# Moving the SBUF addresses of a matmul kernel's operands: the weights' ring to a multiple of 512 bytes, each streamed buffer to an offset of its own

## The chip, the cores and the metric

The kernel is one program on one NeuronCore of a Trainium2 chip. The metric is the device time of one execution in microseconds (us). TensorE (PE) multiplies, ScalarE (ACT), VectorE (DVE) and GpSimd (POOL) do the elementwise work, SyncE (SP) issues most of the transfers.

## What is computed

The reference is two blocks of a small transformer, batch 1, 512 tokens, width 1024, everything in float32. Each of the first two layers does this:

```python
xn = rmsnorm(h, norm_g[i]);  proj = xn @ w_in[i]          # a recurrent mixer and a sparse attention read proj
h = h + concatenate([y_hg, y_nsa]) @ w_out[i]
gate = sigmoid(rmsnorm(h, ple_norm_g[i]) @ w_pg[i])
h = h + gate * (p[i] @ w_pp[i])
```

Then come two layers of the second block, each a feed-forward part, a mixer (differential attention in the first, pooling in the second), a cross attention to a memory of 256 tokens, and a second feed-forward part, with a layer norm after each:

```python
def swiglu_ffn(x, w_in, w_out):                           # D_FF = 2816
    h = x @ w_in
    g, u = jnp.split(h, 2, axis=-1)
    return (jax.nn.silu(g) * u) @ w_out
```

What matters for this change is that nearly all the work is a product of an activation of 512 tokens with a weight matrix, 464 slabs of weights of 128 x 1024 numbers in all.

## The kernel before

Activations lie transposed in SBUF (channel on the partition, token along it). `h` is the running activation, [128, 8, 512]. A float32 product is made as three products of the type float32r: every operand is split into a rounded high part and the low part that is left. The weights go through three rings of RING = 4 slots, 4096 bytes per partition each: SP loads a slab into `raw` (a transfer of 512 KB), ACT rounds it into `wh` (line 883), POOL writes the low part `wl` = raw - wh (line 319), and PE reads `wh` and `wl`. The activations are split into pairs: `xh`, `xl` ([128, 8, 512], the input of most products), `hh`, `hl` ([128, 22, 512], the hidden layer of the feed-forward part), `mh`, `ml` ([128, 8, 256], the memory).

All products go through `passes`, which the profile shows as three lines, L405, L407 and L409. Each issues two matmuls, of the left and the right half of a bank of 512 columns, so the order on PE is six matmuls with 256 moving columns, then the next six:

```python
for n, c in enumerate(parts):      # L405: weights wh, moving xh (or hh, mh)
    nc.tensor.matmul(dst[:, c], high_l, high_r[:, c], start=first and n == 0, stop=False)
for c in parts:                    # L407: weights wh, moving xl (or hl, ml)
    nc.tensor.matmul(dst[:, c], high_l, low_r[:, c], start=False, stop=False)
for n, c in enumerate(parts):      # L409: weights wl, moving xh (or hh, mh)
    out = nc.tensor.matmul(dst[:, c], low_l, high_r[:, c], start=False, ...)
```

Every matmul is led by its own load of 128 columns of weights (LDWEIGHTS, the rows of the engine PEld), which runs beside the matmul ahead of it. Six of these per 128 x 128 tile of weights make 48 per slab. In the stages that produce values with the token on the partition (`token_major`), the roles are swapped: `xh`, `xl`, `mh` or `ml` is the loaded operand, and the ring (`wh`, `wl`) is the streamed one, 256 columns wide or, in one stage of each of the first layers, 280.

The stages are in a fixed order that is written out by hand (`plan`), and engines wait for each other by semaphores. PE, ACT and POOL go two to four slabs ahead of each other within the ring. Between the products lie the stages of the mixers (plain float32 matmuls, other lines) and the norms, in which DVE, ACT and POOL work on `h`, `tb`, `sg`, `sq`, `s1`, `s2` and write `xh` and `xl` again (POOL line 333).

A tensor's place in SBUF isn't given in the code. It follows from the order of the `keep` calls: each tensor starts where the one before it ends, rounded up to 32 bytes, and the first one behind a scratch area of 16384 bytes and 128 bytes of constants. Tensors made by `views` are released again and are laid over by what follows, so `hh`/`hl`, `proj` and what follows it, `dq` and the others, `xq` to `xpt`, and `pooled` all begin at one address. Of each matmul operand the table gives the start (bytes from the partition's start) and what is left of it after division by 512; each slot, each tile of weights (512 bytes) and each half of a bank (1024 bytes) has the same remainder as its buffer.

| buffer | start before | rest of 512 before | start after | rest of 512 after |
|---|---|---|---|---|
| h | 16512 | 128 | 4096 | 0 |
| raw | 32896 | 128 | 20480 | 0 |
| wh | 49280 | 128 | 36864 | 0 |
| wl | 65664 | 128 | 53248 | 0 |
| sg, tb, sq, s1, s2 | 86368 and on | 352 | 73952 and on | 224 |
| xh | 104512 | 64 | 92192 | 32 |
| xl | 120896 | 64 | 108640 | 96 |
| hh | 137280 | 64 | 125568 | 128 |
| hl | 182336 | 64 | 170752 | 256 |
| mh | 178240 | 64 | 166720 | 320 |
| ml | 186432 | 64 | 174976 | 384 |

Of the kernel before, what the change touches and what calls it, by code (L numbers as in the profile page):

```python
# [25 lines left out]
P = 128  # L26
T = 512
TT = T // P
D = 1024
KC = D // P  # L30
DEPTH = 2
NF = 22
MEM = 256
# [131 lines left out]
def program(nc, x_t, slabs, prm1, prm2, consts, rot2, rope, masks, cmp_tab, spread, causal, w1, pp_w, p_t,  # L165
            pool_w, mem_t, positions, out):
    f32, f32r, bf16, i32 = mybir.dt.float32, mybir.dt.float32r, mybir.dt.bfloat16, mybir.dt.int32
# [6 lines left out]
    with ctx:  # L174
        def keep(name, shape, dt=f32):
            return ctx.enter_context(nc.sbuf_tensor(name, shape, dt))
# [2 lines left out]
            return ctx.enter_context(nc.semaphore(name))  # L179


        h = keep("h", [P, KC, T])
        raw = keep("raw", [P, RING, D])
        wh = keep("wh", [P, RING, D], f32r)
# [15 lines left out]
        ksm = keep("ksm", [P, 3, 64])  # L200
        lbt = keep("lbt", [P, 4, 4])
        lam = keep("lam", [P, 4])


        def views(specs):
            made = []
            with ExitStack() as scope:
                for name, shape, dt in specs:
                    made.append(scope.enter_context(nc.sbuf_tensor(name, shape, dt)))
            return made  # L210


        with nc.sbuf_tensor("x_room", [P, 2 * KC * T], f32):
# [9 lines left out]
                                    ("pct", [P, 2, T], f32)])  # L223

        (dpa, dpt) = views([("dpa", [P, 3, 1280], f32), ("dpt", [P, 2, TT, T], f32)])
        xh, xl = keep("xh", [P, KC, T], f32r), keep("xl", [P, KC, T], f32r)

        (proj, vt, vgt, rop, msk, cmt, side, spr) = views([
            ("proj", [P, NPROJ, T], f32), ("vt", [P, TT, T], f32), ("vgt", [P, TT, VG], f32),
# [3 lines left out]
            ("dq", [P, KC, T], f32), ("dk", [P, KC, T], f32), ("dkz", [P, 2, KC, T], f32), ("dv", [P, TT, D], f32),  # L233
            ("drop", [P, 2, T], f32), ("dspr", [16, 8 * P], f32)])
        (dpos,) = views([("dpos", [P, T], i32)])
        (xq, xk, xv, xm, mh, ml, xpa, xpt) = views([
            ("xq", [P, KC, T], f32), ("xk", [P, KC, MEM], f32), ("xv", [P, MT, D], f32),
            ("xm", [P, KC, MEM], f32), ("mh", [P, KC, MEM], f32r), ("ml", [P, KC, MEM], f32r),
            ("xpa", [P, 2, TT, MEM], f32), ("xpt", [P, 2, MT, T], f32)])

        (pooled, _, pside) = views([("pooled", [P, KC, T], f32), ("memory_room", [P, 5 * KC * MEM], f32),
                                    ("pside", [P, 16, P], f32)])
        hh, hl = keep("hh", [P, NF, T], f32r), keep("hl", [P, NF, T], f32r)
        pin = vt
        tot_a = proj[:, KCM:KCM + 2, :].rearrange("p a t -> p (a t)").rearrange("p (h t) -> p h t", h=4)
        tot_b = sq[:, 0, :].rearrange("p (h t) -> p h t", h=4)
# [1725 lines left out]
```

## Time and profile before

| | |
|---|---|
| time, median of 3 runs | 3622.61 us |
| the 3 runs | 3620.0, 3622.61, 3631.73 us |
| the profiled execution's own time | 3616.13 us |
| its span, first to last instruction | 3614.3 us |
| PE busy | 3243.3 us, 90% |
| PEld busy | 2907.5 us, 80% |
| POOL, DVE, ACT busy | 1369.7, 1251.1, 1105.5 us |
| mean granted clock of TensorE | 0.946 of 2.4 GHz |
| moved by DMA | 261.86 MB, 72 GB/s over the span |

The busy time of an engine counts the time in which at least one of its instructions runs. Matmuls overlap in the records, so a matmul's duration (276 ns, say) is longer than the time from its start to the start of the next, and it's this second time that adds up to the span. In a stretch where PE never stops, it's the stretch divided by the number of matmuls.

### The profile page before, as it was taken

The numbers are of one execution on the slowest core, as the hardware profiler recorded it, in microseconds if no ns is written. First come the engines' busy times: TensorE is split into PE (matmuls) and PEld (weight loads), VectorE is DVE, ScalarE is ACT, GpSimd is POOL, SyncE is SP. The second block draws the span as 40 slices with busy tenths as digits, with TensorE's granted clock in tenths as the row PEclk, the third lists the DMA queues.
The fourth block names the chain that finished last, engine by engine and source line by source line (L and its number), as shares of the span: only waits on it lengthen the run. The fifth ranks groups of instructions, "written<-read, shape, count | busy, mean of one in ns | idle before, by whom it ended". The sixth has DMA issues, their size and how long they took to land.

```text
span 3614.3 us, 59291 instructions
## 1 busy us (share of the span) xinstructions
PE 3243.3 (90%) x24262; PEld 2907.5 (80%) x24262; DVE 1251.1 (35%) x2127; ACT 1105.5 (31%) x1835; POOL 1369.7 (38%) x651
## 2 busy tenths in 40 slices
PE   5988898997799899989788898999899987889997
PEld 5985476997358899979447878999799975789997
DVE  2026654106564311050576053110411058251103
ACT  2232433222253322132253333221322233332222
POOL 4433014443103344444403624444444444244442
PEclk9988899998799999999898999999999998999999
DMA  4320012331001232313101412222232331213231
GB/s 160 93 70 18 1 30 76 96 102 36 6 1 59 77 99 93 99 57 105 35 1 58 134 46 74 92 93 96 64 99 93 100 101 57 70 60 101 95 99 53
DMA packets 72068, 261.86 MB, mean 72 GB/s; under 512 B 7920, under 2 KB 8560, under 8 KB 70800
## 3 DMA queue, kind: packets, MB, share of 16 engines
q1 hardware_dynamic: 70048, 250.32, 21.8%
q10 hardware_dynamic: 1904, 9.94, 0.8%
q8 instruction: 79, 1.29, 0.1%
q14 instruction: 37, 0.30, 0.0%
HBM read 258.13 MB, written 2.10 MB: 72 GB/s over the span
## 4 chain that ended last, share of the span: by engine, by line
PE 77%; DVE 15%; ACT 3%; issue 3%; POOL 1%; DMA 0%; SPq 0%; DVEq 0%; ACTq 0%; POOLq 0%
PE bank L405 22%; PE bank L409 21%; PE bank L407 21%; PE bank L644 2%; PE bank L670 2%; DVE tb L1352 1%; PE bank L635 1%; DVE sg L1341 1%; PE bank L582 1%; PE bank L818 1%; DVE s L1302 1%; ACT wh L883 1%; PE bank L576 1%; PE bank L508 1%; DVE proj L1464 1%
## 5 line engine op out<-in xcount | busy, mean ns | idle before, releaser
L319 POOL TENSOR_TENSOR wl<-raw,wh 128x1024 fp32r<-128x1024 f32 x464 | 1153.9, 2503 | 1876.3 <-ACT wh L883 1876.2
L405 PE MATMUL bank<-xh,wh 128*128 128x256 f32 x5120 | 1017.4, 280 | 106.8 <-POOL xl L333 77.6
L407 PE MATMUL bank<-xl,wh 128*128 128x256 f32 x5120 | 1010.5, 279 | 0.0
L409 PE MATMUL bank<-xh,wl 128*128 128x256 f32 x5120 | 1009.7, 279 | 0.0
L405 PEld LDWEIGHTS bank<-xh,wh 128*128 128x128 f32 x5120 | 783.5, 190 | 124.1 <-issue 94.3
L883 ACT CAST wh<-raw 128x1024 fp32r<-128x1024 f32 x464 | 468.3, 1047 | 1043.4 <-PE bank L409 1010.6
L407 PEld LDWEIGHTS bank<-xl,wh 128*128 128x128 f32 x5120 | 783.7, 190 | 0.0
L409 PEld LDWEIGHTS bank<-xh,wl 128*128 128x128 f32 x5120 | 781.9, 190 | 0.0
L405 PE MATMUL bank<-hh,wh 128*128 (+1 forms) x1408 | 279.3, 280 | 5.8 <-ACT sg L1132 5.8
L409 PE MATMUL bank<-hh,wl 128*128 (+1 forms) x1408 | 279.3, 280 | 0.0
L407 PE MATMUL bank<-hl,wh 128*128 (+1 forms) x1408 | 279.0, 280 | 0.0
L1630 DVE TENSOR_TENSOR tb<-sg,bank 128x512 f32<-128x512 f32 x88 | 60.5, 687 | 616.7 <-ACT sg L1132 616.7
L1132 ACT ACTIVATE sg<-bank 128x512 f32<-128x512 f32 x88 | 52.7, 598 | 685.6 <-PE bank L409 685.6
L1584 DVE SCALAR_TENSOR_TENSOR h<-h,bank 128x512 f32<-128x512 f32 x72 | 49.5, 687 | 512.7 <-PE bank L409 511.0
L405 PEld LDWEIGHTS bank<-hh,wh 128*128 128x128 f32 x1408 | 215.3, 189 | 6.5 <-ACT sg L1132 6.5
L409 PEld LDWEIGHTS bank<-hh,wl 128*128 128x128 f32 x1408 | 215.4, 189 | 0.0
L407 PEld LDWEIGHTS bank<-hl,wh 128*128 128x128 f32 x1408 | 214.4, 188 | 0.0
L1632 DVE TENSOR_TENSOR hl<-tb,hh 128x512 f32 x88 | 123.7, 1405 | 161.9 <-ACT hh L1136 161.9
L1546 DVE TENSOR_REDUCE small<-bank 128x1 f32<-128x128 f32 (+1 forms) x224 | 106.7, 476 | 81.3 <-PE bank L645 73.8
L1370 DVE COPY proj<-bank 128x512 f32 x28 | 19.4, 692 | 293.2 <-PE bank L409 293.2
L644 PE MATMUL bank<-proj 128*128 128x128 f32 (+3 forms) x256 | 89.1, 471 | 11.7 <-DVE proj L1513 11.4
L333 POOL TENSOR_TENSOR xl<-h,xh 128x512 fp32r<-128x512 f32 x48 | 73.3, 1538 | 62.2 <-ACT xh L937 61.6
(301 smaller groups left out, 3613.3 us busy)
## 6 DMA issues: line engine op xcount, KB each, us to landing
raw<-in_slabs SPq DMA_DIRECT2D x464, 512.0 KB, 3.5
h<-in_x_t SPq DMA_DIRECT2D x1, 2048.0 KB, 8.4
w1v<-in_w ACTq DMA_DIRECT2D x2, 1024.0 KB, 4.8
side<-in_pp_w ACTq DMA_DIRECT2D x2, 1024.0 KB, 4.8
xm<-in_mem_t ACTq DMA_DIRECT2D x2, 1024.0 KB, 4.8
out<-h SPq DMA_DIRECT2D x8, 256.0 KB, 2.0
side<-in_w SPq DMA_DIRECT2D x1, 1024.0 KB, 14.2
vt<-in_p_t ACTq DMA_DIRECT2D x2, 512.0 KB, 3.6
```

The costliest lines, as they stand in the source:

```text
L319: nc.gpsimd.tensor_tensor(wl[:, n % RING, :], raw[:, n % RING, :], wh[:, n % RING, :], A.subtract).then_inc(w_low, 1)
L333: nc.gpsimd.tensor_tensor(xl[:, c, :], h[:, c, :] if st["kind"] == "ln" else tb[:, c % 2, :], xh[:, c, :], A.subtract).then_inc(S["xl"], 1)
L405: nc.tensor.matmul(dst[:, c], high_l, high_r[:, c], start=first and n == 0, stop=False)
L407: nc.tensor.matmul(dst[:, c], high_l, low_r[:, c], start=False, stop=False)
L409: out = nc.tensor.matmul(dst[:, c], low_l, high_r[:, c], start=False, stop=last and n == len(parts) - 1)
L644: nc.tensor.matmul(bank[t][:, 0:w], q[:, t * P:w], k[:, 0:w], start=True, stop=False)
L670: last = nc.tensor.matmul(o[:, k * P:T], vgt[:, k, col:col + 64], ptt[:, u % 2, k, k * P:T], start=False, stop=(br == 1 and k == TT - 1))
L883: nc.scalar.copy(wh[:, slot, :], raw[:, slot, :]).then_inc(w_high, 1)
L1132: nc.scalar.activation(sg[:, j, :], bank[2 * j][:], F.Silu).then_inc(took_a, 1)
L1546: step(V.tensor_reduce(small[:, 0, u % 2, t:t + 1], bank[t][:, 0:w(t)], AX, A.max))
L1630: V.tensor_tensor(tb[:, j, :], sg[:, j, :], bank[2 * j + 1][:], A.mult).then_inc(took_v, 1)
L1632: V.tensor_tensor(flat(hl[:, bass.ds(i * 2 + j, 1), :]), tb[:, j, :], flat(hh[:, bass.ds(i * 2 + j, 1), :]), A.subtract).then_inc(S["hl"], 1)
```

## The change

No instruction is added, removed or moved on any engine, and no operand changes its shape or type. Only addresses change. The scratch area shrinks from 16384 to 2048 bytes; pads are put ahead of `h` (1920 bytes), behind `lam` (64), ahead of `xh` (32), `xl` (64), `hh` (128), `hl` (128), `mh` (320) and `ml` (64), and behind `xl` (416). The ring and `h` come to multiples of 512, and the six streamed buffers to the six offsets of the table above. The buffers of the mixers (`proj`, `hk`, `dq` and so on) go from 64 to 0 bytes above a multiple of 512.

```diff
+        keep("fore_room", [P, 2048 - 128], mybir.dt.uint8)
         h = keep("h", [P, KC, T])
         raw = keep("raw", [P, RING, D])
         wh = keep("wh", [P, RING, D], f32r)
...
         lam = keep("lam", [P, 4])
+        keep("mid_room", [P, 64], mybir.dt.uint8)
...
-        xh, xl = keep("xh", [P, KC, T], f32r), keep("xl", [P, KC, T], f32r)
+        u8 = mybir.dt.uint8
+        keep("xh_room", [P, 32], u8)
+        xh = keep("xh", [P, KC, T], f32r)
+        keep("xl_room", [P, 64], u8)
+        xl = keep("xl", [P, KC, T], f32r)
+        keep("x_end", [P, 512 - 96], u8)
...
-        (xq, xk, xv, xm, mh, ml, xpa, xpt) = views([
+        (xq, xk, xv, xm, _, mh, _, ml, xpa, xpt) = views([
             ("xq", [P, KC, T], f32), ("xk", [P, KC, MEM], f32), ("xv", [P, MT, D], f32),
-            ("xm", [P, KC, MEM], f32), ("mh", [P, KC, MEM], f32r), ("ml", [P, KC, MEM], f32r),
+            ("xm", [P, KC, MEM], f32), ("mh_room", [P, 320], u8), ("mh", [P, KC, MEM], f32r),
+            ("ml_room", [P, 64], u8), ("ml", [P, KC, MEM], f32r),
...
-        (pooled, _, pside) = views([("pooled", [P, KC, T], f32), ("memory_room", [P, 5 * KC * MEM], f32),
+        (pooled, _, pside) = views([("pooled", [P, KC, T], f32), ("memory_room", [P, 5 * KC * MEM + 96], f32),
...
-        hh, hl = keep("hh", [P, NF, T], f32r), keep("hl", [P, NF, T], f32r)
+        keep("hh_room", [P, 128], u8)
+        hh = keep("hh", [P, NF, T], f32r)
+        keep("hl_room", [P, 128], u8)
+        hl = keep("hl", [P, NF, T], f32r)
...
-    nc = bacc.Bacc("TRN2", target_bir_lowering=False, num_devices=1)
+    nc = bacc.Bacc("TRN2", target_bir_lowering=False, num_devices=1, dynamic_dma_scratch_size=2048)
```

## Rows read from the trace of the kernel before

**Rows 1.** The profile's page: busy times, and the chain that ended last
```profile
PE 3243.3 (90%) x24262; PEld 2907.5 (80%) x24262; DVE 1251.1 (35%) x2127; ACT 1105.5 (31%) x1835; POOL 1369.7 (38%) x651
...
PE 77%; DVE 15%; ACT 3%; issue 3%; POOL 1%; DMA 0%; SPq 0%; DVEq 0%; ACTq 0%; POOLq 0%
PE bank L405 22%; PE bank L409 21%; PE bank L407 21%; PE bank L644 2%; PE bank L670 2%; DVE tb L1352 1%; PE bank L635 1%; DVE sg L1341 1%; PE bank L582 1%; PE bank L818 1%; DVE s L1302 1%; ACT wh L883 1%; PE bank L576 1%; PE bank L508 1%; DVE proj L1464 1%
```

**Rows 2.** Groups on PE: xcount, busy us, mean ns of one, idle before
```profile
L405 PE MATMUL bank<-xh,wh 128*128 128x256 f32 x5120 | 1017.4, 280 | 106.8 <-POOL xl L333 77.6 <-DVE xl L1312 21.4 <-ACT vgt L973 4.5
...
L405 PE MATMUL bank<-hh,wh 128*128 (+1 forms) x1408 | 279.3, 280 | 5.8 <-ACT sg L1132 5.8
...
L405 PE MATMUL bank<-wh,xh 128*128 128x256 f32 (+1 forms) x320 | 72.0, 291 | 22.7 <-POOL xl L333 13.3 <-ACT vt L973 4.5 <-ACT dk L962 2.6
...
L405 PE MATMUL bank<-mh,wh 128*128 128x256 f32 x128 | 38.3, 299 | 20.2 <-POOL ml L393 10.7 <-POOL wl L319 5.7 <-ACT xq L962 3.1
...
L405 PE MATMUL bank<-wh,mh 128*128 128x256 f32 x128 | 27.3, 296 | 6.7 <-ACT xq L962 2.6 <-ACT xk L962 2.4 <-ACT xv L973 1.6
```

**Rows 3.** Windows inside feed-forward stages: length, busy us (xcount), granted clock
```profile
1460.00:1570.00 110.00, 110.00 (x937) 110.00 (x935) 3.00 (x5) 21.24 (x21) 45.77 (x20) 1.00 0.32 98
2200.00:2430.00 230.00, 230.00 (x1955) 230.00 (x1954) 41.79 (x40) 59.97 (x80) 104.08 (x40) 1.00 0.30 93
...
2600.00:2810.00 210.00, 210.00 (x1855) 210.00 (x1855) 40.32 (x39) 58.21 (x78) 98.95 (x38) 1.00 0.30 97
2825.00:2935.00 110.00, 110.00 (x973) 110.00 (x972) 6.25 (x10) 22.24 (x23) 47.08 (x20) 1.00 0.31 100
```

**Rows 4.** Timeline of PE in two stages with the same buffers: start, length
```profile
1499.92 0.40 PE L409 MATMUL bank<-hh,wl 128*128 x2
1500.16 0.40 PE L405 MATMUL bank<-hh,wh 128*128 x2
1500.39 0.40 PE L407 MATMUL bank<-hl,wh 128*128 x2
...
2900.06 0.39 PE L405 MATMUL bank<-hh,wh 128*128 x2
2900.29 0.39 PE L407 MATMUL bank<-hl,wh 128*128 x2
2900.51 0.39 PE L409 MATMUL bank<-hh,wl 128*128 x2
```

**Rows 5.** Windows over the stretches at the longer spacing, PE's count first
```profile
38.70:81.00 42.30, 37.96 (x288) 37.56 (x288) 9.44 (x10) 13.87 (x18) 26.37 (x15) 0.93 0.33 102
500.00:608.00 108.00, 104.02 (x798) 95.80 (x798) 50.12 (x52) 35.54 (x50) 44.65 (x22) 1.00 0.22 69
629.00:672.00 43.00, 38.32 (x291) 37.95 (x292) 9.53 (x10) 13.86 (x18) 27.06 (x16) 0.93 0.35 104
1455.00:1582.00 127.00, 126.54 (x1061) 125.32 (x1062) 16.17 (x23) 26.49 (x30) 50.73 (x21) 1.00 0.28 87
1722.00:1747.00 25.00, 22.88 (x192) 22.68 (x192) 1.38 (x2) 5.21 (x6) 16.49 (x7) 1.00 0.27 85
2047.00:2077.00 30.00, 26.30 (x200) 25.71 (x201) 1.83 (x4) 11.07 (x13) 22.88 (x10) 0.94 0.52 166
2190.00:2432.00 242.00, 240.54 (x2042) 240.37 (x2042) 44.58 (x43) 65.68 (x88) 110.47 (x44) 1.00 0.29 91
2432.00:2560.00 128.00, 127.55 (x1064) 125.68 (x1064) 16.15 (x23) 27.46 (x31) 50.71 (x22) 1.00 0.27 87
3466.00:3594.00 128.00, 127.53 (x1063) 125.83 (x1064) 16.16 (x23) 26.32 (x30) 48.33 (x20) 1.00 0.21 66
```

**Rows 6.** Other matmuls: min/median/max ns; first one with 64 moving columns
```profile
L523 PE MATMUL bank<-prm,hidv x8: 275/275/323, 278.4 to 871.7; 128*128 128x64 f32 x8
...
L635 PE MATMUL bank<-cst,pa x320: 272/273/329, 393.2 to 1087.5; 128*128 128x128 f32 x160
```

**Rows 7.** Two stretches of one token-major stage, where the roles are swapped
```profile
L409 PE MATMUL bank<-wh,xl 128*128 128x256 f32 x59 | 11.6, 276 | 0.0
...
L405 PE MATMUL bank<-wh,xh 128*128 128x256 f32 x62 | 12.4, 281 | 2.2 <-ACT dv L973 2.2
```

**Rows 8.** The ring's work, its waits and its transfers
```profile
L319 POOL TENSOR_TENSOR wl<-raw,wh 128x1024 fp32r<-128x1024 f32 x464 | 1153.9, 2503 | 1876.3 <-ACT wh L883 1876.2
...
L883 ACT CAST wh<-raw 128x1024 fp32r<-128x1024 f32 x464 | 468.3, 1047 | 1043.4 <-PE bank L409 1010.6
...
L333 POOL TENSOR_TENSOR xl<-h,xh 128x512 fp32r<-128x512 f32 x48 | 73.3, 1538 | 62.2 <-ACT xh L937 61.6
...
raw<-in_slabs SPq DMA_DIRECT2D x464, 512.0 KB, 3.5
```

## The prediction

> **What bounds the kernel now.** I read the page first. The chain that ended last is PE for 77%, and three lines, L405, L407 and L409, hold 64% of it [rows 1]. The groups of PE say what these are: 5120 + 1408 + 320 + 128 + 128 = 7104 matmuls on each of the three lines, 21,312 in all, nearly all with 256 moving columns, a mean duration of 280 ns, and little idle time ahead of them [rows 2]. So next I asked how far apart they start. In a window in which PE is busy throughout, that's length over count. The first and the last window of [rows 3] both lie inside a stage that makes the output of a feed-forward part: the same code, the same buffers `hh`, `hl`, `wh`, `wl`, the same granted clock of 1.00. Yet one has 937 matmuls in 110 us (117.4 ns each), the other 973 (113.1 ns). The timeline shows the same thing as a steady pace: two matmuls in 0.235 us in the first, in 0.225 us in the second [rows 4]. The two windows between them give 230 / 1955 = 117.6 and 210 / 1855 = 113.2 ns for the stages that read `xh` and `xl` [rows 3]. There are two levels, 4.4 ns apart, and a stage stays on one for hundreds of matmuls, up to two thousand.
>
> Most of the longer level lies in the nine stretches of [rows 5]. Their counts add up to 288 + 798 + 291 + 1061 + 192 + 200 + 2042 + 1064 + 1063 = 6999, about one third of the 21,312. They hold a few others, and a few short stretches are not in them, which I leave out. So the longer level costs 7000 x 4.4 = **31 us** now, and the other 14,300 would cost **63 us** more if they were on it too.
>
> Everything else about the ring is covered. POOL waits 1876 us for ACT, ACT 1011 us for PE, and a slab's load lands in 3.5 us, where PE takes 48 x 113 ns = 5.4 us for a slab, with four slots between them [rows 8].
>
> **The change, part by part.** No instruction comes or goes, so no term comes from a count. There are four terms, each a changed duration.
>
> *The products with the ring as weights* (5120 + 1408 + 128 on each line, 94% of the 21,312). Before, the two operands that PE reads at a time lie at 128 and 64 bytes above a multiple of 512. They are the same in every stage, and both levels occur with them. So the addresses alone don't select the level; what PE did before must. What the trace can't show is what happens at other distances, as it has only one here. It bears on it in one place: in the token-major stages the roles are swapped, and with them the sign of the distance (the loaded operand at 64, the streamed one at 128). There the durations are 276 and 281 ns, again within one stage [rows 7], and 276 and 281 are what the two levels give in the products. A distance of +64 behaves as one of -64. The change makes the distance (streamed minus ring) 32, 96, 128, 256, 320 and 384. The bounds for this term:
> - Below: the matmul with 64 moving columns still takes 275 ns [rows 6], when its streaming is a quarter as long. Something other than the streaming sets that, and the load of 128 columns of weights is what it shares with the 256-column ones. 275 against 276 leaves 1 ns, with rounding up to 1.7 ns per matmul. The 128-column transposes at 272 ns [rows 6] are a different kind of load, and I don't count on them. So the most that a change of address could give is all on the lower level, 31 us, and 21,312 x 1.6 = 34 us below it, 65 us in all.
> - Above: all on the longer level, +63 us. A third level further up is possible, but none of the 256-column rows shows one.
>
> My value lies between. At present all operands of a stage have equal remainders, so the six matmuls of `passes` repeat with nothing that differs, and a stage that starts at the longer level has nothing that could bring it out (1061, 1064 and 1063 matmuls in a row, [rows 5]). With `xh` and `xl` 64 bytes apart, and `hh` and `hl` 128, the sequence has two changes in six. That can end a bad pace, or a good one. As two thirds are on the lower level now, it seems the more easily reached of the two. And the loaded and the streamed operand come further apart for all but `xh` (32). I take it that a bit more than half of what is lost on the longer level comes back: the share falls from 33% to 15%, or 3800 matmuls x 4.4 ns = **-17 us**.
>
> *The token-major products* (6%, 1344 matmuls): the streamed ring is at 0, the weights at 32, 96, 320, 384. The same bounds, -1 to +6 us; 0 taken.
>
> *The work on DVE, ACT and POOL*: their operands go from 128, 64 and 352 to 0 and the like, 224, 32 and 96. Nothing in the trace ties a duration to an address. POOL's `xl` takes 1538 ns [rows 8], and PE waits 77.6 us in all for it [rows 2]. A change of 10% either way in all of them is 7 us; 0 taken. If `wl` (2503 ns) took 10% more, it would still be hidden: two slabs take 5.5 us of POOL and 10.9 of PE.
>
> *Transfers*: `raw` goes to a multiple of 512. The ring's loads are hidden by the two loads that are ahead. 0. The shorter scratch area takes nothing away, as no queue of POOL's moves data.
>
> The sum is -17 us. Against the profiled execution it's 3616 - 17 = 3599; that one is 6.5 us below the median of the three runs, so against the median it's 3622.6 - 17 = **3606 us**.
>
> **What the skill says to this.** [...] The Trainium skill, "SBUF — State Buffer", section "Who interferes with whom", has PE with two independent read ports, and says "PE and ACT never wait on anyone"; its section on operand start alignment asks only for a multiple of the element's size, and adds that this is about legality and that nothing was timed. By this rule both layouts are alike and the time is 3622.6: it's the first rival below. [...]
>
> **The rivals.**
> - *Addresses don't matter* (0.30). For it: both levels at equal addresses, and no change with the sign of the distance. Then each stage draws its level anew from how it starts. A stage like the feed-forward output is 1063 x 4.4 = 4.7 us either way, so a few of them give +-10 us, about the spread of the three runs (11.7 us). Time 3622, between 3612 and 3633.
> - *The unequal offsets keep knocking PE off the lower level* (0.28). This is the case on the slower side. The lower level needs equal conditions from one matmul to the next, it's now held for 1855 matmuls in a row [rows 3], and a change of remainder twice in six ends it. All at the longer level gives 3622.6 + 63 = 3685; half of the lower ones gives 3654. It decides as soon as the share at the longer level is over 45%, where it's 33% now: each tenth of the 21,312 is 9.4 us, and 0.3% of the time (about what a measurement of this kernel can tell from no change) is 11 us.
> - *Below the lower level* (0.10): the new distances remove what's left above the weights' load. 3622.6 - 65 = 3558, if everywhere.
> - The forecast itself (0.32): 3591 with all on the lower level to 3611.
>
> **How the numbers follow.** The chance of faster by over 0.3% is 0.32 + 0.10 = 0.42, of slower 0.28, of no change 0.30. The likeliest case is 3606, its own range 3591 to 3611. As cases of both signs hold much, the range goes from 3560, where the lower rival is nearly whole, to 3676, close to the end of the upper one, and leaves some 0.07 below and 0.09 above it.
>
> **What the profile of the changed kernel would show.** Right: the mean duration of the L405, L407 and L409 groups falls from 280 towards 277 ns, and the windows of feed-forward stages hold 970 matmuls in 110 us, not 937, in at least three of the four. The groups with `xh`, `hh` and `mh` may then differ from each other, as they have different offsets; were they alike, the offset would not be the cause. If addresses don't matter, windows of both counts are seen again, at other places, and the means stay near 280. If unequal offsets hurt, windows of 937 are all over, or there is a pace between the two. A mean below 276 would be the third case. What would make me wrong in another way: a duration on DVE or POOL that moves by over 5%, a ring that no longer keeps up (PE waiting for `wl` L319, which it does for next to nothing now), or a changed granted clock.

## The result, and the profile after

The changed kernel takes **3676.6 us** (median of 4 runs, 3674.98 to 3680.52), against 3627.17 for the kernel before in the same rounds (3620.0 to 3647.14). The ratio is 1.0129, interval 1.0086 to 1.0172 (it compares all the runs, so it isn't the quotient of the two medians): slower by 1.3%. The forecast of 3606 has the wrong sign, and the time lies 0.6 us above the end of the range. The profiled execution is 3674.98 us with a span of 3673.2, 58.9 us more than before.

The page of the changed kernel: busy times, the chain by engine, and the groups that answer to [rows 2] and [rows 8] (xcount, busy us, mean ns | idle before). The edits move the three lines of the products from L405, L407, L409 to L416, L418, L420.

```profile
PE 3305.6 (90%) x24262; PEld 2969.6 (81%) x24262; DVE 1248.7 (34%) x2127; ACT 1105.0 (30%) x1835; POOL 1369.0 (37%) x651
...
PE 76%; DVE 15%; issue 4%; ACT 3%; POOL 1%; DMA 0%; SPq 0%; DVEq 0%; ACTq 0%; POOLq 0%
...
L330 POOL TENSOR_TENSOR wl<-raw,wh 128x1024 fp32r<-128x1024 f32 x464 | 1152.9, 2501 | 1935.1 <-ACT wh L894 1935.1
L416 PE MATMUL bank<-xh,wh 128*128 128x256 f32 x5120 | 1030.3, 283 | 104.6 <-POOL xl L344 76.1
...
L416 PE MATMUL bank<-hh,wh 128*128 (+1 forms) x1408 | 281.5, 281 | 5.8 <-ACT sg L1143 5.8
```

Only PE has changed: 3243.3 before [rows 1], 3305.6 now, which is 62.3 us more of a span that grew by 58.9. DVE, ACT and POOL have moved by 2.4 us at most; `wl` takes 2501 ns where it took 2503 [rows 8]; PE's wait for `xl` is 76.1 us where it was 77.6 [rows 2]. The 59 us that POOL waits longer for ACT are PE's, handed on through the ring.

The windows inside three stages (length, PE busy with its count) answer to [rows 3]: the first is a feed-forward output, the second reads `xh` and `xl`, the third is the output that was at the lower level before.

```profile
1490.00:1600.00 110.00, 110.00 (x934) 110.00 (x933) 7.54 (x11) 21.42 (x22) 43.02 (x18) 1.00 0.28 91
2620.00:2830.00 210.00, 208.42 (x1770) 208.21 (x1769) 39.20 (x39) 58.41 (x78) 96.38 (x38) 1.00 0.29 90
2870.00:2980.00 110.00, 110.00 (x933) 110.00 (x933) 2.64 (x4) 21.20 (x21) 45.70 (x20) 1.00 0.32 98
```

No feed-forward stage holds 973 any more: 110 / 933 is 117.9 ns and 208.42 / 1770 is 117.8. (A window also counts the two or three matmuls that run across its edges, so the quotient comes out some 0.2 ns below the distance of the starts: 110 / 973 is 113.1 where the starts are 113.3 apart.) The clock is 1.00 as before, so this is no throttle. The timeline shows what a pace of this kind looks like inside (start, length of a pair):

```profile
1300.06 0.40 PE L416 MATMUL bank<-xh,wh 128*128 128x256 f32 x2
1300.29 0.40 PE L418 MATMUL bank<-xl,wh 128*128 128x256 f32 x2
1300.53 0.41 PE L420 MATMUL bank<-xh,wl 128*128 128x256 f32 x2
```

Taken one matmul at a time it isn't the old longer level. These are the distances from one start to the next, in ns, in a stage with `xh` and `xl`, in the kernel before and in the changed one (differences of start times, 18 of each):

```
before  118 117 118 118 117 119 117 118 118 118 117 118 118 117 119 117 118 118
after   116 117 117 128 120 115 120 115 116 118 118 116 117 118 117 116 119 117
```

Before, the steps are even. After, they are uneven (115 to 128), the 18 repeat as a group, and they sum to 2120 ns, a mean of 117.78. The old longer level sums to 2120 too, so the mean alone doesn't tell the two apart.

### The profile page after: what moved, and what is told of

Same layout as the page of the kernel before. It is cut to its first block, busy times and chain, and to the rows that moved or that the text cites. A ratio compares the mean times of both kernels' runs of the same rounds, so it can differ in the third digit from the quotient of the medians.

```text
span 3673.2 us, 59291 instructions
## 1 busy us (share of the span) xinstructions
PE 3305.6 (90%) x24262; PEld 2969.6 (81%) x24262; DVE 1248.7 (34%) x2127; ACT 1105.0 (30%) x1835; POOL 1369.0 (37%) x651
## 4 chain that ended last, share of the span: by engine, by line
PE 76%; DVE 15%; issue 4%; ACT 3%; POOL 1%; DMA 0%; SPq 0%; DVEq 0%; ACTq 0%; POOLq 0%
PE bank L420 21%; PE bank L416 21%; PE bank L418 21%; PE bank L655 2%; PE bank L681 2%; DVE tb L1363 1%; PE bank L646 1%; DVE sg L1352 1%; PE bank L593 1%; ACT wh L894 1%; PE bank L829 1%; PE bank L587 1%; DVE s L1313 1%; PE bank L519 1%; DVE proj L1475 1%
## 5 line engine op out<-in xcount | busy, mean ns | idle before, releaser
L330 POOL TENSOR_TENSOR wl<-raw,wh 128x1024 fp32r<-128x1024 f32 x464 | 1152.9, 2501 | 1935.1 <-ACT wh L894 1935.1
L416 PE MATMUL bank<-xh,wh 128*128 128x256 f32 x5120 | 1030.3, 283 | 104.6 <-POOL xl L344 76.1
L420 PE MATMUL bank<-xh,wl 128*128 128x256 f32 x5120 | 1036.3, 284 | 0.0
L418 PE MATMUL bank<-xl,wh 128*128 128x256 f32 x5120 | 1020.9, 281 | 0.0
L416 PEld LDWEIGHTS bank<-xh,wh 128*128 128x128 f32 x5120 | 795.2, 190 | 122.6 <-issue 96.3
L420 PEld LDWEIGHTS bank<-xh,wl 128*128 128x128 f32 x5120 | 790.8, 190 | 0.0
L418 PEld LDWEIGHTS bank<-xl,wh 128*128 128x128 f32 x5120 | 789.2, 190 | 0.0
L416 PE MATMUL bank<-hh,wh 128*128 (+1 forms) x1408 | 281.5, 281 | 5.8 <-ACT sg L1143 5.8
L420 PE MATMUL bank<-hh,wl 128*128 (+1 forms) x1408 | 281.4, 282 | 0.0
L418 PE MATMUL bank<-hl,wh 128*128 (+1 forms) x1408 | 279.7, 280 | 0.0
L416 PEld LDWEIGHTS bank<-hh,wh 128*128 128x128 f32 x1408 | 216.1, 188 | 6.5 <-ACT sg L1143 6.5
L418 PEld LDWEIGHTS bank<-hl,wh 128*128 128x128 f32 x1408 | 216.2, 188 | 0.0
L420 PEld LDWEIGHTS bank<-hh,wl 128*128 128x128 f32 x1408 | 215.0, 189 | 0.0
```

The costliest lines, as they stand in the source:

```text
L330: nc.gpsimd.tensor_tensor(wl[:, n % RING, :], raw[:, n % RING, :], wh[:, n % RING, :], A.subtract).then_inc(w_low, 1)
```

## The experiments

All change addresses alone, by the size of pads. xl_alone and wl_alone have the remainders of the kernel before, but the changed kernel's short scratch area and its place for the mixers' buffers; wl128_only alone is built on the kernel before, all others on the changed one. "Distance" is the start of the streamed operand minus that of the loaded one. Remainders are those by 512. `passes` reads (`wh`, `xh`), (`wh`, `xl`) and (`wl`, `xh`), two matmuls of each in turn. The pace is window length over count, or the mean difference of start times inside a stage where no window is shown (differences of 150 ns and more, which are waits, left out). It's that of the profiled execution; where this one lies at an end of a kernel's runs, the text says so. The x, h and m stages are those that stream `xh`/`xl`, `hh`/`hl` and `mh`/`ml`. There are 18 x stages, four h stages (feed-forward outputs) and two m stages, and between them six token-major ones. The layouts, and what they took (the four scans and odd16 have two runs each):

| kernel | wh, wl | xh, xl | hh, hl | mh, ml | median us | ratio to before, interval |
|---|---|---|---|---|---|---|
| changed | 0, 0 | 32, 96 | 128, 256 | 320, 384 | 3676.6 | 1.0129 [1.0086, 1.0172] |
| equal_pairs | 0, 0 | 32, 32 | 128, 128 | 320, 320 | 3671.0 | 1.0106 [1.0051, 1.0160] |
| all_zero | 0, 0 | 0, 0 | 0, 0 | 0, 0 | 3714.0 | 1.0226 [1.0171, 1.0281] |
| xl_alone | 128, 128 | 64, 128 | 64, 64 | 64, 64 | 3661.5 | 1.0110 [1.0075, 1.0145] |
| wl_alone | 128, 192 | 64, 64 | 64, 64 | 64, 64 | 3656.6 | 1.0090 [1.0057, 1.0123] |
| scan_a | 0, 0 | 256, 256 | 192, 192 | 384, 384 | 3699.6 | 1.0200 [1.0101, 1.0300] |
| scan_b | 0, 0 | 160, 160 | 96, 96 | 480, 480 | 3697.4 | 1.0194 [1.0099, 1.0290] |
| scan_c | 0, 0 | 224, 224 | 384, 384 | 352, 352 | 3687.6 | 1.0167 [1.0071, 1.0263] |
| scan_d | 0, 0 | 64, 64 | 288, 288 | 416, 416 | 3666.2 | 1.0108 [1.0013, 1.0203] |
| odd16 | 0, 0 | 80, 80 | 48, 48 | 64, 64 | 3704.6 | 1.0215 [1.0153, 1.0277] |
| all_64 | 0, 0 | 64, 64 | 64, 64 | 64, 64 | 3664.0 | 1.0104 [1.0056, 1.0151] |
| all_192 | 0, 0 | 192, 192 | 192, 192 | 192, 192 | 3623.5 | 1.0001 [0.9972, 1.0029] |
| same_class | 0, 0 | 64, 192 | 64, 320 | 64, 448 | 3666.5 | 1.0110 [1.0065, 1.0155] |
| wl_class | 0, 128 | 64, 64 | 64, 192 | 192, 64 | 3600.7 | 0.9931 [0.9911, 0.9951] |
| wl128_64 | 0, 128 | 64, 64 | 64, 64 | 64, 64 | 3588.0 | 0.9883 [0.9846, 0.9920] |
| wl128_192 | 0, 128 | 192, 192 | 192, 192 | 192, 192 | 3588.3 | 0.9884 [0.9847, 0.9920] |
| wl128_only | 128, 256 | 64, 64 | 64, 64 | 64, 64 | 3586.9 | 0.9880 [0.9843, 0.9916] |

The first theory behind the result was that of the slower rival: inequality within a streamed pair does it. The first rival to it: the distance does it.

**equal_pairs**: the distances of `xh`, `hh` and `mh` stay, and each pair becomes equal.

```diff
         xh = keep("xh", [P, KC, T], f32r)
-        keep("xl_room", [P, 64], u8)
         xl = keep("xl", [P, KC, T], f32r)
...
         hh = keep("hh", [P, NF, T], f32r)
-        keep("hl_room", [P, 128], u8)
         hl = keep("hl", [P, NF, T], f32r)
```

> The new layout with the two buffers of each pair at one offset again: xh and xl at 32, hh and hl at 128, mh and ml at 320 bytes, the ring at 0. Theory (the unequal offsets inside a pair knock TensorE off its repeating pace): both levels of the kernel before return, stages at 113.3 or 117.8 ns from start to start, each constant over a stage, and the time is 3600 to 3640 us. Rival 1 (the distance from the ring sets the pace): the stages stay near 117.8 (xh) and 118.1 (hh) with matmuls of unequal spacing, time 3670 to 3680. Rival 2 (the move of the other buffers, the scratch area or h costs it): 3670 to 3680 too, but with the even spacing of the kernel before.

3671.0 us (3669.75 to 3672.8). The windows are of an x stage, an h stage and another x stage:

```profile
100.00:200.00 100.00, 100.00 (x859) 100.00 (x859) 6.22 (x9) 22.32 (x27) 42.14 (x19) 1.00 0.30 94
1500.00:1590.00 90.00, 90.00 (x761) 90.00 (x760) 2.27 (x4) 17.02 (x17) 37.17 (x16) 1.00 0.30 93
...
2250.00:2400.00 150.00, 150.00 (x1276) 150.00 (x1275) 28.50 (x27) 38.98 (x52) 70.87 (x28) 1.00 0.30 92
```

100 / 859 is 116.4 and 90 / 761 is 118.3; from the start times the first two stages have 116.7 and 118.67. The lower level doesn't return, and the theory that inequality alone does it falls. The h stages are slower than any h or x stage before. The third window, 150 / 1276, lies in an x stage at 117.8 by its start times: thirteen of the 18 x stages have 116.7 or 116.8, five 117.6 to 117.8. So a distance of 32 has two paces too, and a stage draws one of them.

**all_zero**: every remainder 0.

```diff
-        keep("xh_room", [P, 32], u8)
         xh = keep("xh", [P, KC, T], f32r)
-        keep("xl_room", [P, 64], u8)
         xl = keep("xl", [P, KC, T], f32r)
-        keep("x_end", [P, 512 - 96], u8)
```

> Everything at a multiple of 512 bytes: the ring and all six streamed buffers at 0, so that the distance is nothing and the offsets are equal. Theory (only unequal offsets cost): two even levels, 3600 to 3640 us, as with equal pairs. Rival (the distance from the ring matters by itself, and two operands at one offset collide most): a level above 118 ns in all products, 3690 us or more.

3714.0 us (3713.5 to 3715.07), the slowest of all. Window of an x stage, one of an h stage, and one of a later x stage:

```profile
100.00:200.00 100.00, 100.00 (x836) 100.00 (x835) 6.23 (x9) 21.55 (x26) 39.28 (x18) 1.00 0.31 94
...
1500.00:1600.00 100.00, 100.00 (x836) 100.00 (x835) 0.00 (x0) 18.85 (x18) 41.33 (x18) 1.00 0.31 96
2300.00:2400.00 100.00, 100.00 (x835) 100.00 (x835) 17.50 (x17) 25.90 (x35) 43.32 (x18) 1.00 0.31 94
```

They are 119.6 and 119.8 (100 / 836 and 100 / 835), and the starts are 120 ns apart, even to the nanosecond in most stages. With nothing unequal, distance 0 alone costs 6.7 ns a matmul over the lower level.

**xl_alone and wl_alone**: the ring at 128 and the streamed buffers at 64, as before, but `xl` or `wl` shifted by 64 bytes. The lines show that shift alone, for both kernels; the pads that keep the other buffers at their remainders are left out.

```diff
         xh = keep("xh", [P, KC, T], f32r)
+        keep("xl_room", [P, 64], mybir.dt.uint8)     # xl_alone
         xl = keep("xl", [P, KC, T], f32r)
...
         wh = keep("wh", [P, RING, D], f32r)
+        keep("wl_room", [P, 64], mybir.dt.uint8)     # wl_alone
         wl = keep("wl", [P, RING, D], f32r)
```

> The offsets of the kernel before (ring 128, all streamed buffers 64), and xl alone 64 bytes further, at 128, which is also the ring's own offset. Theory: the products on xh and xl go to a mean of 117.8 ns with uneven spacing at once, those on hh and hl stay on 113.3 or 117.8 with even spacing; time 3655 to 3675 us. Rival (distance): only the line that streams xl changes its pace, and the time moves by a third of that.

> The offsets of the kernel before, and wl alone 64 bytes further, at 192, so that the streamed buffers keep equal offsets and only the loaded ones differ, two of six in each repeat. If the load's address takes part in the pace, the products leave the two even levels, as with unequal streamed buffers: 3650 us or more. If only the streamed operand's address does, the products stay on 113.3 or 117.8 ns, only the token-major stages (6% of the matmuls), which stream wh and wl, change, and the time is 3600 to 3640 us.

3661.5 (10 runs, 3651.64 to 3668.29) and 3656.6 (10 runs, 3654.51 to 3658.42). With `xl` shifted, every x stage is at 117.24 and uneven, and the h stages, whose addresses relative to the ring are those of before, have 113.35 three times and 117.78 once. (The profile is that of the fastest of the ten runs, 10 us under their median; two h stages more on the longer level would be 9 us, so the other runs may have fewer on the lower one.) With `wl` shifted, x and h stages all have 116.7. Window of an h stage of each, xl_alone's first:

```profile
1480.00:1590.00 110.00, 110.00 (x973) 110.00 (x972) 6.07 (x10) 21.30 (x21) 48.16 (x20) 1.00 0.33 101
```

```profile
2460.00:2570.00 110.00, 110.00 (x946) 110.00 (x945) 4.87 (x8) 21.10 (x21) 45.31 (x19) 1.00 0.31 96
```

The loss follows the shifted buffer, and a shift of a loaded operand costs the lower level as one of a streamed operand does. So it's the relation of the two that counts, not where the streamed buffer lies by itself.

**The scan (scan_a to scan_d, odd16)**: pairs equal, ring at 0, so each stage measures one distance. The edit is the pad ahead of the pair; scan_a's is shown, the others differ in the numbers of the table (odd16 starts each tile 16 bytes in).

```diff
-        keep("xh_room", [P, 32], u8)
+        keep("xh_room", [P, 256], mybir.dt.uint8)
...
-        keep("hh_room", [P, 128], u8)
+        keep("hh_room", [P, 192], mybir.dt.uint8)
...
-            ("xm", [P, KC, MEM], f32), ("mh_room", [P, 320], u8), ("mh", [P, KC, MEM], f32r),
-            ("ml_room", [P, 64], u8), ("ml", [P, KC, MEM], f32r),
+            ("xm", [P, KC, MEM], f32), ("mh_room", [P, 384], u8), ("mh", [P, KC, MEM], f32r),
+            ("ml_room", [P, 512], u8), ("ml", [P, KC, MEM], f32r),
```

> The ring at 0 and equal offsets inside each pair: xh, xl at 256, hh, hl at 192, mh, ml at 384. Distance theory, as it stands after the first four runs (the pace is a function of streamed minus loaded offset modulo 512: 120.0 ns at 0, 116.7 at 32, 118.7 at 128, 113.3 or 117.8 at +64 and -64, 117.8 at 320, 113.3 at 192): each pair has one pace of its own in all its stages; the hh stages at 192 have 113.3, with some stages at 117.8; xh at 256, the furthest there is, at or below 113.3. Rival (colliding only near 0, the rest is how a stage starts): all three pairs at 113.3 or 117.8.

> As before with xh, xl at 160, hh, hl at 96, mh, ml at 480. Distance theory: 96 and 160 lie between neighbours at 113.3 to 118.7 and are odd multiples of 32, as 32 is, which had an uneven pace of 116.7 to 117.6: 116 to 118 ns for both, in every stage. Rival: 113.3 or 117.8 by stage.

> As before with xh, xl at 224, hh, hl at 384, mh, ml at 352. Distance theory: 384 is -128; if the sign doesn't matter, as it didn't for 64, 118.7 ns; 224 an odd multiple of 32, 116 to 118 ns. Rival: 113.3 or 117.8 by stage.

> As before with xh, xl at 64, hh, hl at 288, mh, ml at 416. Distance theory: xh at 64 has the two levels of the kernel before (there -64 in the products and +64 in the token-major stages), 113.3 and 117.8 by stage; 288 an odd multiple of 32, 116 to 118 ns. Rival (the ring's or h's own place, not the distance): xh at 64 is uneven too.

> Ring at 0, equal pairs at offsets that are odd multiples of 16 bytes, which the padding of the allocator never gives: xh, xl at 80 and hh, hl at 48, beside the cheap 64 (mh, ml at 64). If the pace depends on the distance in steps of 16 bytes with a minimum at 64, both lie between their neighbours (48 between 116.7 and 113.3, 80 between 113.3 and 120.0). If the steps are 32 or 64 bytes, 80 equals 64 and 48 equals 32. A pace below 113.3 is open: no run has looked there.

Several of these expectations missed: 256 has 120.0 and not 113.3 or less, 96 has 120.0 and 160 up to 118.7 where 116 to 118 was expected, and 48 lies above both its neighbours. Paces by distance, with the stage that gave each ("or" where the stages of one distance fall on two paces):

| distance | pace, ns | and 256 further | pace, ns |
|---|---|---|---|
| 0 | 120.0 (all_zero) | 256 | 120.0 (scan_a x) |
| 32 | 116.7 or 117.8 (equal_pairs x) | 288 | 116.7, once 117.8 (scan_d h) |
| 48 | 118.3 (odd16 h) | | |
| 64 | 113.3 or 117.8 (all_64) | 320 | 117.8 to 117.9 (equal_pairs m) |
| 80 | 118.3 or 120.0, some between (odd16 x) | | |
| 96 | 120.0 (scan_b h) | 352 | 120.0 to 120.1 (scan_c m) |
| 128 | 118.67 (equal_pairs h) | 384 | 118.67 (scan_c h) |
| 160 | 117.3 in three stages, 118.5 to 118.8 in the rest (scan_b x) | 416 | 118.1 to 118.8 (scan_d m) |
| 192 | 113.3 or 117.8 (all_192) | | |
| 224 | 118.3 (scan_c x) | 480 | 118.3 to 118.4 (scan_b m) |

To read two of them off the profile, a window in an x stage of scan_a (distance 256, 100 / 835 = 119.8) and of scan_b (distance 160, 100 / 855 = 117.0, one of the three stages at 117.3):

```profile
100.00:200.00 100.00, 100.00 (x835) 100.00 (x835) 5.67 (x9) 20.09 (x25) 40.14 (x17) 1.00 0.31 95
```

```profile
100.00:200.00 100.00, 100.00 (x855) 100.00 (x854) 6.23 (x9) 22.32 (x27) 41.48 (x19) 1.00 0.30 94
```

In every pair 256 apart the two agree within what a distance scatters by itself (320 was seen in two short stages alone). So what counts is the distance modulo **256**, not 512. The cheap ones are 64 and 192; the kernel before had 64 - 128, which is 192 by this measure, and the change left it for 32, 96, 128 and 256 in the x and h stages. No distance went below 113.3.

In all of these the ring is at 0, so the streamed buffer's own place would fit them as well. The token-major stages settle it, as there the ring is streamed and the buffer loaded, and the distance changes its sign. Windows of the token-major stage ahead of the differential attention: scan_a (distance 0 - 256), scan_c (0 - 224, which is 32) and scan_d (0 - 64, which is 192):

```profile
1740.00:1760.00 20.00, 20.00 (x169) 20.00 (x169) 0.00 (x0) 3.14 (x3) 7.72 (x4) 1.00 0.35 104
...
1729.00:1749.00 20.00, 20.00 (x174) 20.00 (x173) 0.00 (x0) 3.15 (x3) 8.84 (x4) 1.00 0.36 106
...
1750.00:1770.00 20.00, 20.00 (x179) 20.00 (x178) 0.00 (x0) 3.16 (x3) 14.24 (x6) 1.00 0.26 80
```

From the start times they have 119.9, 116.7 and 113.4, the paces of 0, 32 and 192 in the table. The others agree: 0 - 384 (128) has 118.7, 0 - 416 (96) 120.0, 0 - 32 (224) 118.3. So it's the streamed operand's start minus the loaded one's, whichever buffer plays which part.

**all_64 and all_192**: is 64 as good as 192?

```diff
-        keep("xh_room", [P, 32], u8)
+        keep("xh_room", [P, 64], mybir.dt.uint8)     # all_64; 192 in all_192
         xh = keep("xh", [P, KC, T], f32r)
-        keep("xl_room", [P, 64], u8)
         xl = keep("xl", [P, KC, T], f32r)
```

> The new layout in every way (ring and h at 0, short scratch area, all pads) but with all six streamed buffers at 64. Theory (what costs the time is the distance of the streamed from the loaded operand, modulo 256 bytes, and 64 and 192 are its cheapest values): each stage is back on 113.3 or 117.8 ns, evenly, and the time is that of the kernel before within its own scatter, 3594 to 3650 us. Rival (something else of the layout costs part of it): above 3655 us.

> The new layout with all six streamed buffers at 192, that is 64 bytes below the ring's offset modulo 256, as in the kernel before, where all at 64 was 64 above it. If the sign decides how often a stage lands on the upper level (products at -64: a third of the matmuls in the kernel before; at +64, in the run with all at 64: nearly all), the products on xh and xl are at 113.3 ns in most stages and the time is that of the kernel before, 3600 to 3645 us. If the sign doesn't matter and something else of the new layout does, the time is near 3664 us, as with all at 64.

3664.0 us (4 runs, 3659.38 to 3671.38) and 3623.5 (10 runs, 3613.97 to 3641.96): the ranges don't touch. Both levels occur in each, but all_64 draws the longer one in 16 of 18 x stages and three of four h stages, all_192 the lower one in half of its x stages and three of four h stages. The time of all_64 is the one that its rival named, that something else of the new layout costs; all_192 rules that out. Two h stages of all_192 and one of all_64 (110 / 973 = 113.1, 110 / 937 = 117.4):

```profile
1470.00:1580.00 110.00, 110.00 (x973) 110.00 (x972) 6.49 (x10) 22.58 (x23) 46.39 (x20) 1.00 0.32 100
...
2450.00:2560.00 110.00, 110.00 (x937) 110.00 (x936) 2.25 (x5) 21.18 (x21) 46.62 (x20) 1.00 0.32 100
```

```profile
1480.00:1590.00 110.00, 110.00 (x936) 110.00 (x935) 2.85 (x5) 21.17 (x21) 46.06 (x20) 1.00 0.31 98
```

all_192 has the changed kernel's smaller scratch area, its ring at 0 and its moved mixers' buffers, and its time is that of before (1.0001 [0.9972, 1.0029]). So the rest of the change costs nothing beyond some 0.3%.

**same_class and wl_class**: inequality with cheap distances alone. In same_class `xh` and `xl` are at 64 and 192, `hh` and `hl` differ by 256. In wl_class the loaded pair is at 0 and 128, with an equal x pair and an unequal h pair.

```diff
         xh = keep("xh", [P, KC, T], f32r)
-        keep("xl_room", [P, 64], u8)
+        keep("xl_room", [P, 128], mybir.dt.uint8)    # same_class; none in wl_class
         xl = keep("xl", [P, KC, T], f32r)
...
         wh = keep("wh", [P, RING, D], f32r)
+        keep("wl_room", [P, 128], mybir.dt.uint8)    # wl_class alone
         wl = keep("wl", [P, RING, D], f32r)
```

> Ring at 0, unequal pairs whose distances are all cheap ones: xh 64 and xl 192, hh 64 and hl 320, mh 64 and ml 448. Knocking theory (unequal offsets cost by themselves): xh/xl leave the two even levels, 116 to 118 ns in all stages; hh/hl differ by 256 bytes, the period of the distance, so they stay on 113.3 or 117.8. Time 3640 to 3670 us. Pure distance theory: both pairs stay on 113.3 or 117.8 by stage, time 3594 to 3650 us.

> wh at 0 and wl at 128, xh and xl at 64, hh 64 and hl 192, mh 192 and ml 64, so that every streamed operand is 64 bytes above or below every loaded one, modulo 256. Pure distance theory: 113.3 or 117.8 ns in every stage, 3594 to 3650 us. Knocking theory: uneven spacing everywhere, a mean near 116.7 as with wl alone, 3650 to 3670 us. An outcome below 113.3 or with no stage at 117.8 would be a way to gain.

3666.5 us (4 runs, 3661.57 to 3666.7) and 3600.7 (10 runs, 3598.77 to 3614.03). Both profiles are of a run at the end of its range: same_class's of the fastest, 5 us under the median, wl_class's of the slowest, 13 us above it. Two h stages of same_class, then an x stage and an h stage of wl_class:

```profile
1485.00:1595.00 110.00, 110.00 (x936) 110.00 (x935) 5.21 (x8) 20.48 (x21) 45.30 (x19) 1.00 0.30 95
...
2470.00:2580.00 110.00, 110.00 (x973) 110.00 (x972) 8.12 (x12) 22.06 (x23) 45.58 (x19) 1.00 0.32 96
```

```profile
2200.00:2400.00 200.00, 200.00 (x1767) 200.00 (x1766) 37.88 (x37) 54.03 (x72) 96.33 (x37) 1.00 0.31 97
...
1460.00:1570.00 110.00, 110.00 (x936) 110.00 (x936) 3.05 (x5) 21.18 (x21) 45.95 (x20) 1.00 0.31 98
```

In same_class every x stage has 117.8 in uneven steps (114 to 122), as in the changed kernel, although each distance by itself can have 113.3; its h stages, equal modulo 256, have 113.3 in three of four. So inequality does keep PE off the lower level: the slower rival was half right. And wl_class, meant as the mirror of it, showed something else: with `wl` 128 bytes off `wh` and an equal streamed pair, every x stage of the kernel has the lower level (200 / 1767 = 113.2; 113.3 to 114.1 by the starts), while its unequal h pair has 117.5 (110 / 936; 117.8 in uneven steps by the starts) in all four stages of the profiled run. As the median run is 13 us faster, that needn't be so in every run. Its m stages, whose streamed pair is unequal the other way round (192 and 64), have 120.9, more than distance 0 gives; why isn't known.

The token-major stages of same_class are the same case with the roles swapped, `xh` and `xl` loaded, 128 bytes apart, and an equal streamed ring. They are on the lower level throughout, 113.7 from the start times where all the matmuls are 256 columns wide; this is the one that has 119.4 in the changed kernel:

```profile
1750.00:1770.00 20.00, 20.00 (x179) 20.00 (x178) 0.00 (x0) 3.17 (x3) 14.26 (x6) 1.00 0.25 80
```

**wl128_64, wl128_192 and wl128_only**: the loaded pair 128 apart, every streamed pair equal. The first two are on the changed kernel; the third is the kernel before with two pads and nothing else.

```diff
         wh = keep("wh", [P, RING, D], f32r)
+        keep("wl_room", [P, 128], mybir.dt.uint8)
         wl = keep("wl", [P, RING, D], f32r)
...
         lam = keep("lam", [P, 4])
+        keep("lam_end", [P, 512 - 128], mybir.dt.uint8)
```

> wh at 0, wl at 128, all six streamed buffers at 64 (equal pairs). The run with hh at 64 and hl at 192 had every product on xh and xl at 113.4 ns and every product on hh and hl at 117.8. Theory (loaded operands 128 bytes apart and streamed ones equal leave the lower level as the only stable pace): the four feed-forward output stages also go to 113.4, 4224 matmuls by 4.4 ns or 19 us less than that run: 3575 to 3590 us. Rival (what helped was something of the xh buffers' own place): hh and hl stay at 117.8, 3600 us.

> The mirror image: wh at 0, wl at 128, all six streamed buffers at 192, so that wh is the one at a distance of -64 and wl at +64 (modulo 256). If only the loaded operands' being 128 apart counts: all products at 113.4 ns, 3575 to 3590 us. If the order of the signs over the six matmuls counts (four with wh, two with wl): another pace, or two levels again.

> The kernel before with one pad: wl 128 bytes further (256 above a multiple of 512, wh at 128, all streamed at 64), and 384 bytes behind lam to keep all that follows at its offsets. Distances -64 for wh, +64 for wl modulo 256, as in the mirror image. Theory: all products at 113.4 ns in every stage, 3575 to 3595 us, and less scatter between runs than the kernel before (3594 to 3651). Rival: the two levels stay, 3594 to 3650 us.

3588.0, 3588.3 and **3586.9 us** (3585.69 to 3587.54): 1.2% faster than the kernel before, and the changed kernel stands 3676.6 / 3586.9 = 2.5% above it. The groups of wl128_only, then its windows in three h stages and two x stages:

```profile
L407 PE MATMUL bank<-xh,wh 128*128 128x256 f32 x5120 | 1012.9, 279 | 105.5 <-POOL xl L335 76.4
L409 PE MATMUL bank<-xl,wh 128*128 128x256 f32 x5120 | 1007.3, 278 | 0.0
...
L407 PE MATMUL bank<-hh,wh 128*128 (+1 forms) x1408 | 274.3, 276 | 5.8 <-ACT sg L1134 5.8
```

```profile
2200.00:2430.00 230.00, 228.54 (x2016) 228.38 (x2016) 43.01 (x42) 63.04 (x83) 109.33 (x43) 1.00 0.31 99
2620.00:2830.00 210.00, 208.55 (x1841) 208.38 (x1840) 36.68 (x36) 56.26 (x73) 100.70 (x39) 1.00 0.31 97
...
1455.00:1565.00 110.00, 110.00 (x973) 110.00 (x973) 6.04 (x10) 21.82 (x22) 47.34 (x20) 1.00 0.32 101
2415.00:2525.00 110.00, 110.00 (x973) 110.00 (x972) 6.07 (x10) 21.27 (x21) 48.23 (x20) 1.00 0.33 101
2800.00:2910.00 110.00, 110.00 (x973) 110.00 (x972) 6.08 (x10) 21.29 (x21) 48.35 (x21) 1.00 0.32 101
```

All stages with the ring as weights have 113.3 to 114.0 from the start times (the window at 2415 us lies in the stage that [rows 5] has at 2432 us, on the longer level), and the hh group is at 276 ns where it was 280. PE's busy time is 3214.5 us, 28.8 under before. By the start times, 26 us of it come from the x and h stages, and the token-major ones give back 2, as the ring that they stream is now the unequal pair (117.7 to 118.0, and 121.8 where a third of the matmuls is 280 columns wide). The rest lies in the mixers' stages, whose PE time differs by some us from one profile to the next. The other two kernels have the same paces, but for the two short m stages of wl128_64, each of which holds the lower level in its first half and 118.9 in uneven steps in its second, after a wait. So another pace exists even in this layout; it was seen in these 192 matmuls alone. The runs now lie within 2 us; those of the kernel before, which draws a level in each stage, spread over 51 us in the rounds of this study (3594 to 3645, and one at 3651).

## Why the prediction was wrong

*What held.* PE bounds the kernel, and start-to-start spacing, not duration or idle time, is what to read. The two levels of 113.3 and 117.8 ns and their price are confirmed from both sides: the changed kernel, with none of its x and h stages at the lower one, has 62.3 us more PE time (63 forecast for "all at the longer level"), and wl128_only, with all x and h stages on the lower, 28.8 less (31 forecast). The second agreement is in part luck: by the start times the products give 24 us. The count of 7000 holds 579 matmuls of the two token-major stages at 121.0, a third of them 280 columns wide, and these stages came below 118 in no layout. A further slip is in the base. The 31 and the 63 us were read off the profiled execution (3616) and then counted from the median (3622.6), so "all lower" is 3585 and not 3591, and "all longer" 3679 and not 3685; measured were 3586.9 and, for the changed kernel's profiled execution, 3675.0. The terms set to 0 for DVE, ACT, POOL and the transfers are 0 within what can be measured, by the page and by all_192; the token-major term, set to 0 within -1 to +6, is +2.4 us by the start times. Nothing came below the lower level in seventeen layouts, so the lower bound's extra 34 us isn't there for any layout that was tried.

*The step that failed* is the choice inside the first term, "the share falls from 33% to 15%", put at -17 us; the lower level was lost in every stage and PE's time rose by 62.3. It rested on three sentences, and each is wrong:
- "So the addresses alone don't select the level". They don't at a distance of 192 or 64, the only ones that the trace before had. At the others that were tried 113.3 doesn't exist: each distance modulo 256 has one pace or two of its own, all between 116.7 and 120.0 (equal_pairs, all_zero, the scan). What a stage draws is one of the paces that its addresses allow.
- "[T]he sequence has two changes in six. That can end a bad pace, or a good one. As two thirds are on the lower level now, it seems the more easily reached of the two." It only ends the good one: same_class has 117.8 in every x stage. That two thirds were on the lower level said nothing of where an unequal pair leads.
- "And the loaded and the streamed operand come further apart for all but `xh` (32)." Further isn't better: only the remainder by 256 counts, and 256 is the same as 0.

"A distance of +64 behaves as one of -64" was right about which durations occur and wrong about how often: 3664.0 (all_64) against 3623.5 (all_192).

*The rivals.* "Addresses don't matter" falls with all_zero at 3714.0, 1.0226 [1.0171, 1.0281]. What the Trainium skill says in "SBUF — State Buffer", section "Who interferes with whom", that PE's two read ports are independent and PE never waits on anyone, would make all layouts alike, and the measurement decides against that: two whose PE work is instruction for instruction the same differ by 3714.0 - 3586.9 = 127 us. Whether it's at a read port that PE loses the time, no run here shows. "Unequal offsets keep knocking PE off" gave 3685 for all at the longer level, 8 us off, or 4 with the base put right. Its mechanism is one of two: inequality alone gives 3666.5 (same_class, 1.0110 of before), distance alone 3671.0 (equal_pairs, 1.0106), and the changed kernel has both, at 3676.6 (1.0129). They don't add, as each leads to a pace of 117 to 118 where the lower level was. The three token-major stages with `xh` and `xl` rose as well, from 121.0, 121.1 and 115.6 ns to 122.9, 122.3 and 119.4, within the 6 us that the prediction allowed them.

*The size of the range.* "A third level further up is possible, but none of the 256-column rows shows one" was used to leave it out. There are such paces (118.67, 120.0), and all_zero lies at 3714, outside the range altogether. The changed kernel's h stages have 118.2.

*Left open.* Why 256 bytes, why an unequal streamed pair hurts and a loaded pair 128 apart helps, and what draws the level in a stage at a distance with two paces. The pace of a mixed pair isn't the mean of its distances' paces: xl_alone has distances 192 (two matmuls in three) and 0 (one in three), which would give 115.6 at the lower level, and has 117.24.

## What to carry to other kernels

When PE streams without waits, measure its pace as window length over count, stage by stage; two paces for the same instructions and clock are a reserve that neither idle times nor the chain show. The relative start of the two operands modulo 256 bytes is then worth a scan with one pad per stage: 64 or 192 here, never 0 or 96, with the streamed buffers of a stage equal modulo 256. Profile more than one run of a kernel that draws its paces, or check that the profiled run lies near the median. A steady state that a layout only sometimes finds may be made all but the only one (here by 128 bytes between two loaded buffers), which takes the scatter away with the time.

## What the runs showed of the hardware

The time of a float32r matmul of 128 x 128 by 256 columns, start to start, with its weights' load beside it, was between 113.3 and 120.9 ns on the mean of a stage at a granted clock of 1.00. Where the operands start sets which paces a stage can have, and at 32, 64, 80, 160 and 192 there are two. Several paces lie on a grid: 113.33, 116.67, 117.78 and 120.0 are 17, 17 1/2, 17 2/3 and 18 times 6.67 ns (16 cycles at 2.4 GHz), and the 18 uneven steps of the changed kernel sum to 2120 ns, 318 times it. 117.78 is what the longer level has, evenly, at equal offsets, and what the changed kernel, same_class and the h stages of wl_class have as the mean of uneven steps. The duration that the profile gives to one matmul (276 to 286 ns) moved with it, but is over twice the spacing and shows a change of 4% (113.3 to 117.8) as one of 2% (276 to 281).
